# Second attention taken by pairs of heads, its output chunks moved behind all query, key and value chunks

## The reference, cut to what matters

```
def _chunk_attention(h, w_in, rel_bias, w_out):
    q, k, v = jnp.split(h @ w_in, 3, axis=-1)          # 16 heads of 64
    ...
    for each chunk of 64 queries, over a band of its own and the 8 chunks before it:
        s = einsum(q, k) * 64 ** -0.5 + bias           # relative bias, then a mask
        p = softmax(s)
        o = einsum(p, v)
    return o @ w_out
```

## Time and profile before

| | |
|---|---|
| median of 3 runs | 2123.19 us (2122.43 to 2123.32) |
| the profiled execution's own time | 2123.3 us |
| its span, first to last instruction | 2121.5 us |
| PE busy | 2039.8 us, 96% of the span |
| DVE, ACT, POOL busy | 937.8, 769.7 and 935.2 us (44%, 36%, 44%) |
| mean granted clock of TensorE | 0.986 of full speed |

### The profile page before, as it was taken

One profiled execution on the slowest core, in us unless ns is written; L12 is line 12 of the kernel. 1 busy time (PEld: TensorE's weight loads), 2 busy tenths in 40 slices (PEclk: granted clock), 3 DMA queues, 4 the chain that ended last, 5 costly groups with the idle time before them and its releaser, 6 DMA issues.

```text
span 2121.5 us, 24830 instructions
## 1 busy us (share of the span) xinstructions
PE 2039.8 (96%) x9710; PEld 1702.8 (80%) x9710; DVE 937.8 (44%) x1413; ACT 769.7 (36%) x1108; POOL 935.2 (44%) x680
## 2 busy tenths in 40 slices
PE   6988989999997999999999999999999989999998
PEld 5767768888886788888887888888888878888886
DVE  5477372323236754545545131325445555132233
ACT  5256442232233442424244232223444444232232
POOL 4440345555454435353535454555332214455552
PEclk9999999999998999999999999999999999999999
DMA  5340137466322323131322333323223203332321
GB/s 156 97 129 6 60 65 122 102 107 112 99 81 79 100 80 99 61 99 59 99 63 96 100 99 99 99 85 112 84 77 96 79 21 99 99 99 91 94 92 59
DMA packets 170016, 188.58 MB, mean 89 GB/s; under 512 B 4168, under 2 KB 158544, under 8 KB 169808
## 3 DMA queue, kind: packets, MB, share of 16 engines
q1 hardware_dynamic: 167648, 182.07, 26.9%
q10 hardware_dynamic: 1904, 4.59, 4.3%
q0 software_dynamic: 384, 0.81, 0.2%
HBM read 180.77 MB, written 4.72 MB: 87 GB/s over the span
## 4 chain that ended last, share of the span: by engine, by line
PE 71%; issue 15%; POOL 9%; DVE 3%; ACT 2%; DMA 0%; SPq 0%; POOLq 0%; ACTq 0%; DVEq 0%
PE ps L557 23%; PE ps L559 22%; PE ps L558 22%; POOL w_lo L527 9%; PE ps L708 1%; PE ps L719 1%; DVE hn_lo L1491 0%; DMA o_buf<-in_x 0%; PE ps L592 0%; DVE scr L1466 0%; PE ps L966 0%; DVE x L1840 0%; DVE hn_lo L1845 0%; ACT w_hi L977 0%; DVE scr L1698 0%
## 5 line engine op out<-in xcount | busy, mean ns | idle before, releaser
L527 POOL TENSOR_TENSOR w_lo<-raw,w_hi 128x512 fp32r<-128x512 f32 x652 | 916.9, 1437 | 1142.0 <-ACT w_hi L977 1142.0
L557 PE MATMUL ps<-hn_hi,w_hi 128*128 128x512 f32 x1504 | 600.4, 399 | 25.6 <-DVE hn_lo L1491 10.5
L559 PE MATMUL ps<-hn_hi,w_lo 128*128 128x512 f32 x1504 | 589.3, 392 | 0.0
L977 ACT ACTIVATE w_hi<-raw 128x2048 fp32r<-128x2048 f32 x163 | 312.4, 1917 | 762.9 <-PE ps L559 755.6
L558 PE MATMUL ps<-hn_lo,w_hi 128*128 128x512 f32 x1504 | 589.0, 392 | 0.0
L557 PE MATMUL ps<-hid_hi,w_hi 128*128 128x512 f32 x920 | 362.1, 394 | 5.3 <-issue 1.5
L557 PEld LDWEIGHTS ps<-hn_hi,w_hi 128*128 128x128 f32 x1504 | 284.4, 189 | 100.0 <-issue 22.1
L559 PE MATMUL ps<-hid_hi,w_lo 128*128 128x512 f32 x920 | 359.1, 390 | 0.0
L558 PE MATMUL ps<-hid_lo,w_hi 128*128 128x512 f32 x920 | 359.0, 390 | 0.0
L558 PEld LDWEIGHTS ps<-hn_lo,w_hi 128*128 128x128 f32 x1504 | 284.7, 189 | 61.4 <-issue 3.8
L559 PEld LDWEIGHTS ps<-hn_hi,w_lo 128*128 128x128 f32 x1504 | 284.5, 189 | 60.1
(11 more groups left out here) (222 smaller groups left out, 1986.8 us busy)
## 6 DMA issues: line engine op xcount, KB each, us to landing
raw<-in_mlp_w SPq DMA_DIRECT2D x64, 1024.0 KB, 5.3
raw<-in_ret_w_in SPq DMA_DIRECT2D x24, 1024.0 KB, 5.2
raw<-in_att_w_in SPq DMA_DIRECT2D x12, 1024.0 KB, 5.3
raw<-in_w_gate SPq DMA_DIRECT2D x11, 1024.0 KB, 5.4
raw<-in_w_up SPq DMA_DIRECT2D x11, 1024.0 KB, 5.4
raw<-in_w_in SPq DMA_DIRECT2D x8, 1024.0 KB, 5.7
raw<-in_w_down SPq DMA_DIRECT2D x8, 1024.0 KB, 8.7
raw<-in_ret_w_out SPq DMA_DIRECT2D x8, 1024.0 KB, 5.1
```

What stands on the lines that cost most here:

```text
L527: ins = pool.tensor_tensor(w_lo[:, slot, at], raw[:, slot, at], w_hi[:, slot, at].bitcast(F32), ALU.subtract)
L557: pe.matmul(o, hi, rhs_hi, start=start, stop=False, skip_group_check=True)
L559: return pe.matmul(o, lo, rhs_hi, start=False, stop=stop, skip_group_check=True)
L977: act.activation(w_hi[:, c.slot, :], raw[:, c.slot, :], ACT.Copy).then_inc(s["w_hi_ready"], 1)
```

## The change

The output chunks move behind all others: q0 k0 v0 q1 k1 v1 q2 k2 v2 q3 k3 v3 o0 o1 o2 o3. The heads are worked in pairs, eight pairs. The 14 chunks from v0 on are cut into 56 quarters of twelve matmuls of 512 columns (24 of 256 in a value chunk); pair p has its six phases ahead of the quarters 3 + 6p to 8 + 6p:

| phase | PE, ahead of that quarter |
|---|---|
| 0 | scores of the tiles 3, 2, 0 of both heads |
| 1 | scores of tile 1 of both heads |
| 2 | nothing |
| 3 | transposes of the first head |
| 4 | values of the first head, transposes of the second |
| 5 | values of the second head |

The two heads of a pair stand on partitions 0 to 63 and 64 to 127, and their score matmuls take turns, each into a bank of its own. In the values a head's weights are now its high part in 64 columns and its low part in the other 64, so that two matmuls a tile are made where there were three; the two halves of the result have to be added, by an ACT copy to the other half's partitions (`pair_shift`) and a DVE addition (`pair_sum`). ACT and DVE have their steps, the splits of the chunks among them, in the order of the phases. The biases are loaded two heads at a time. The scaled queries and keys go to `rstd` and to the place of `ext`, so that `scr` is free for the scores of two heads; some outputs go to `probs_t` and `hn_hi`. The first attention is as it was.

```diff
-ATT_ORDER = [(kind, g) for kind, g in zip("qkvqkvqkvoqkvooo", (0, 0, 0, 1, 1, 1, 2, 2, 2, 0, 3, 3, 3, 1, 2, 3))]
+ATT_ORDER = [(kind, g) for kind, g in zip("qkvqkvqkvqkvoooo", (0, 0, 0, 1, 1, 1, 2, 2, 2, 3, 3, 3, 0, 1, 2, 3))]
+ATT_FIRST, ATT_EVERY = 3, 6
+        EARLY, LATE = (3, 2, 0), (1,)
# TensorE
+            def pair_scores(p, tiles):
+                a = PAIRS[p]
+                if tiles is EARLY and a.half == 0:
+                    pe.wait_ge(s["att_in_lo"], a.group * 4 + 4)
+                for t in tiles:
+                    if tiles is LATE:
+                        pe.wait_ge(s["two_mx"], 8 * p + 2)
+                    elif p and t == 3:
+                        pe.wait_ge(s["two_lo"], 8 * p)
+                    elif p and t == 2:
+                        pe.wait_ge(s["two_o"], 2 * p)
+                    for n in range(3):
+                        for b in range(2):
+                            q, k = a.qk(b)[n]
+                            ins = pe.matmul(a.score_ps(b, t), q[:, t * P:(t + 1) * P], k[:, 0:(t + 1) * P],
+                                            start=(n == 0), stop=(n == 2), skip_group_check=True)
...
+            def pair_values(p, b):
...
+                for n, (j, subtracted) in enumerate(V_ORDER[b]):
+                    pe.wait_ge(s["two_lo"], 8 * p + 4 * b + subtracted)
+                    o, v = a.out_ps(b)[:, j * P:], a.v_both(b, j)
+                    pe.matmul(o, v, a.pt(0, j), start=(n == 0), stop=False, skip_group_check=True)
+                    ins = pe.matmul(o, v, a.pt(1, j), start=False, stop=(n == 3), skip_group_check=True)
...
+            for quarter in range(ATT_QUARTERS):
+                p, phase = pair_at(quarter)
+                if 0 <= p < ATT_PAIRS:
+                    if phase == 0:
+                        pair_scores(p, EARLY)
+                    if phase == 1:
+                        pair_scores(p, LATE)
+                    if phase == 3:
+                        pair_transposes(p, 0)
+                    if phase == 4:
+                        pair_values(p, 0)
+                        pair_transposes(p, 1)
+                    if phase == 5:
+                        pair_values(p, 1)
+                att_quarter(2 + quarter // 4, quarter % 4)
# ScalarE
+                if phase == 0 and p and p != 6:
+                    pair_out_hi(p - 1)
+                if phase == 1:
+                    if even:
+                        group_ready(ATT.group(ATT.upto[j]))
+                        take(j)
+                    pair_exps(p, 0)
+                    pair_exps(p, 1)
+                if phase == 3:
+                    pair_prob_hi(p, 0)
+                    if p == 6:
+                        pair_out_hi(5)
+                    next_split(quarter - 2 if even else quarter)
+                if phase == 4:
+                    pair_prob_hi(p, 1)
+                    if not even:
+                        take(1 + (quarter - 1) // 4)
+                if phase == 5:
+                    pair_shift(p, 0)
+                    pair_shift(p, 1)
+                    if even:
+                        next_split(quarter)
+                        take(j)
# VectorE
+                if phase != 1 and phase != 4:
+                    add_quarter(quarter - 1)
+                if phase == 0:
+                    pair_masked(p, EARLY)
+                if phase == 1:
+                    pair_masked(p, LATE)
+                    pair_negated(p, 0)
+                    pair_negated(p, 1)
+                    if p and p != 6:
+                        pair_out_lo(p - 1)
+                    take(j)
+                    add_quarter(quarter - 1)
+                if phase == 2:
+                    pair_probabilities(p, 0)
+                if phase == 3:
+                    if not even:
+                        scale(j)
+                    pair_prob_lo(p, 0)
+                    if p == 6:
+                        pair_out_lo(5)
+                    pair_probabilities(p, 1)
+                if phase == 4:
+                    pair_prob_lo(p, 1)
+                    if not even:
+                        take(1 + (quarter - 1) // 4)
+                    add_quarter(quarter - 1)
+                if phase == 5:
+                    if even:
+                        scale(j)
+                    pair_sum(p, 0)
+                    pair_sum(p, 1)
```

More of the change, by code:

```diff
@@ L930, in _ @@
-            att_product(0, act_wait=normed(N_ATT))
+                    if n == 0:
+                        pe.wait_ge(s["two_olo"], 2 * four + 2)
+                    g = ATT.group(ATT.upto[j] + n)
+                    hi, lo = (ap[:, c.slot, :].rearrange("p (k c) -> p k c", k=2) for ap in (w_hi, w_lo))
+                    group_empty(g)
+                    for k, a in enumerate(PAIRS[2 * four:2 * four + 2]):
+                        for m in range(2):
+                            at = slice((2 * n + m) * P, (2 * n + m) * P + P)
+                            ins = three(ps[:, g.bank(m), :], hi[:, k, at], lo[:, k, at], a.out(0), a.out(1),
+                                        k == 0, k == 1)
@@ L931, in _ @@
+                    ins.then_inc(s["group_done"], 1)
+                else:
+                    product(c, g, KD, 256, 0, hn_hi, hn_lo, None, range(2 * n, 2 * n + 2), n == 0, n == 3)
+            chunk_ready(ATT.chunk(0))
+            product(ATT.chunk(0), ATT.group(0), KD, 256, 0, hn_hi, hn_lo, normed(N_ATT))
             stat_columns(N_ATT)
             stat(N_ATT)
[L933 to L960, removed]
+            chunk_ready(ATT.chunk(1))
@@ new lines, in _ @@
+            product(ATT.chunk(1), ATT.group(1), KD, 256, 0, hn_hi, hn_lo)
+            for quarter in range(ATT_QUARTERS):
[13 more added lines that the diff above has]
+                att_quarter(2 + quarter // 4, quarter % 4)
@@ L1436, in _, with pair_exps @@
             take(1)
[L1437 to L1446, removed]
+            def pair_exps(p, b):
+                a = PAIRS[p]
+                act.wait_ge(s["two_nmx"], 2 * p + b + 1)
+                for t in range(4):
+                    col = slice(4 * b + t, 4 * b + t + 1)
+                    act.activation(a.score_sb(b, t), a.score_sb(b, t), ACT.Exp, bias=nmx[:, col],
+                                   accum_out=sm[:, col]).then_inc(s["two_exp"], 1)
@@ new lines, in pair_out_hi, with next_split @@
+            def pair_out_hi(p):
+                if p == 5:
+                    act.wait_ge(s["group_done"], ATT.group(ATT.upto[ATT_ORDER.index(("v", 3))]).done)
+                act.wait_ge(s["two_o"], 2 * p + 2)
+                act.activation(PAIRS[p].out(0), o_sum, ACT.Copy).then_inc(s["two_ohi"], 1)
+            def next_split(quarter):
+                j = 1 + quarter // 4
+                group_ready(ATT.group(ATT.upto[j + 1] - 1))
+                split(ATT.chunk(j + 2) if j < 14 else MLP_B.chunk(0))
@@ new lines, in _ @@
+            for quarter in range(ATT_FIRST, ATT_FIRST + ATT_EVERY * ATT_PAIRS):
+                p, phase = pair_at(quarter)
+                j = 1 + quarter // 4
+                even = p % 2 == 0
+                if phase == 0 and p and p != 6:
[21 more added lines that the diff above has]
+                        take(j)
@@ L2064, in _ @@
+            pair_out_lo(ATT_PAIRS - 1)
+            for quarter in range(ATT_FIRST + ATT_EVERY * ATT_PAIRS - 1, ATT_QUARTERS - 4):
+                add_quarter(quarter)
             for n in range(4):
```

317 lines of the change are left out of this document (206 added, 111 removed).

## The result

| | before | after |
|---|---|---|
| median | 2122.81 us (4 runs, 2122.12 to 2123.32) | 2085.81 us (4 runs, 2083.77 to 2088.40) |
| ratio after to before | | 0.9827, 95% interval 0.981 to 0.9844 |
| span of the profiled execution | 2121.5 us | 2083.8 us |
| k0 to the second MLP | 265.8 us, clock 0.98 | 227.7 us, clock 1.00 |

The kernel is 37.0 us faster by the medians and 37.7 by the spans. The attention is 38.1 us shorter; the rest of the span is 0.4 longer.

The account below looks back on a forecast made before the run. The prediction took PE, busy 96% of the span, as the bound. Its terms -13.7 - 10.2 - 9.2 + 1 + 3 = -29.1 us took 2123.3 to a forecast of 2094 us, range 2084 to 2107.

Parts of the forecast that it names:

- tail: Attention's last part, from 1695.43 on: waits and half clock of four heads with little beside them would go, -13.7 us.
- values: Value matmuls on PE: two for three in each key tile, 0.64 us a head over sixteen heads, -10.2 us.
- scores: Score matmuls of a pair's two heads, taking turns between row halves: partly side by side, -9.2 us.
- case B: Scores: matmuls side by side, weight loads one after another, 3.1 us a pair, saving 9.2 us; chance 0.38.
- insertions: Attention work enters the products 40 times instead of 32, each about 0.1 us late: +1 us.
- new waits: PE waiting in the pairs' new order: 0.3 us a pair plus one delay of 0.8, +3 us.
- Case A: Scores: both heads fully side by side, 2.3 us a pair, saving 15.4 us, time 2088; chance 0.24.
- C: Scores: nothing side by side, 4.2 us a pair, saving nothing, time 2103.4; chance 0.20.
- Rival 3: Attention: the softmax chain becomes the bound, waits of 18.4 us in place of 3, time 2109.6; chance 0.12.
- Rival 4: Scores: changing halves drains PE, 0.19 us for each of 192 matmuls, 36.5 us, time 2139.9; chance 0.04.
- The signs: Attention stretch 230 to 243 us, clock 1.00, no PE wait above 1 us, eight value matmuls a head in about 1.35.

Follow-up runs that it names:

- e3: The changed kernel with the last head's values after quarter 51 instead of before quarter 50, so nothing stands between them and output chunk o3; 2092.14 us.
- e2: The changed kernel with a third matmul for each key tile in the values, the low part once more; 2093.84 us.
- e1: The changed kernel with all of the first head's score matmuls in a section before all of the second's, without turns; 2097.91 us.
- e6: The changed kernel with the second head's scores reading the first head's 64 partitions, turns and banks kept; 2100.51 us.
- e4: The changed kernel with the transposes of a pair's first head one quarter earlier, in phase 2; 2129.39 us, ratio 1.0048 to the kernel before the change.
- e1b: The changed kernel with score matmuls tile by tile, three of the first head and then three of the second; 2084.82 us.
- e5: The changed kernel with, in pair 6, the low part of pair 5's output made after the second head's probabilities instead of before; 2083.87 us.
- e8: The changed kernel with POOL making only the first of the four parts of every low weight chunk; 2068.79 us.

## Why the prediction was right, step by step

| term | predicted | measured |
|---|---|---|
| tail | -13.7 | -13.7, by the idle time and clock that are gone |
| values | -10.2 | 16 x (1.27 - 1.99) = -11.5 |
| scores | -9.2 (case B) | 16 x 2.12 to 8 x 2.27: -15.8 |
| insertions | +1 | +1.9, by the starts of the products |
| new waits | +3 | +1.0 |
| sum | -29.1 | -38.1; the attention -38.1, the span -37.7 |

- **Tail.** Right: the attention's clock is 1.00 in both parts, and e3 shows what a chain without cover costs.
- **Values.** Right. The spacing gave 0.64 a head (e2: the same). The other 0.08 is the change to the 64-row form, which used to follow each head's values and now follows a product: e2's three matmuls a tile take 1.90 us without it, where they took 1.99.
- **Scores.** That the halves run side by side was right, and the size was off: the step that failed is "Two loads make 0.22 a step", with its 3.1 us a pair. Two loads and two matmuls of 128 columns fit in 0.11 us, and a pair takes 2.27. The spacing of matmuls on one half bounds that half alone. Case A, the first rival, is what happened: 2.27 us a pair against its 2.3, and with it the forecast would have been 2088. The prediction gave A 0.24 and B 0.38. Also, its "8 x 1.1 = 9.2" does not come out as printed: 8 x 1.1 is 8.8, and from 4.24 - 3.07 it is 9.4, which moves the forecast by under 0.5 us. The Trainium skill (TensorE: Matmul & The Clock Gate, Part 3: Packing small matmuls) says that matmuls on different row groups run at the same time and that their weight loads overlap; the x2 rows of the changed kernel agree, loads included. In the same section the Trainium skill says that matmuls start and end strictly in program order; the row at 1536.91 of e1 does not agree, and the measurement decides.
- **Insertions.** Too small by 0.9: after a score section the twelve matmuls take 2.94 us and after values or transposes 2.85, where twelve alone take 12 x 0.227 = 2.72. Of the 1.9 us 0.8 lie in the value chunks, which the prediction did not look at.
- **New waits.** The slack ahead of the first head's transposes was put at 0.7 us and at nothing in case A. Case A happened, and the probabilities still end 0.7 to 0.8 us ahead in six pairs (0.06 in two): the softmax chain starts at the end of the late scores, so it comes earlier together with PE, and faster scores take nothing from the slack. The one delay beside the output chunks was put at 0.8 us and is 0.86 to 1.0, but not by the additions that the prediction named: a low part of an output stands ahead of the multiplications there, and the last of them is held up by POOL. That the sizes agree is luck.
- **Rivals.** C is out by e6. Rival 3 did not happen, but its price was too low: e4, one quarter away from the change, is slower than the kernel before it. The prediction priced a lost slack at 18.4 us; e4 shows 46.5, since a shifted order also meets POOL. Rival 4, a drain at each change of halves, is out: 24 changes a pair cost nothing in sight. The 0.31 us between heads 12 and 13 fit the wait for DVE, as the weight load of that matmul shows:
```profile
1700.65 0.18 PEld L708 LDWEIGHTS ps<-hid_hi 64*128 64x128 f32 x1 [0.24 <-DVE small L1698]
```
- **The signs.** Of what would show it right, the clock, the largest wait (0.86 us) and the eight value matmuls (1.27 us a head) came as said. The stretch from k0 to the MLP did not: 227.7 us, below the 230 to 243. The time was inside its range because the range had been drawn to hold case A; the forecast itself was 8 us off, most of it in the scores.

## What to carry to other kernels

Matmuls with a contraction of 64 ran two at a time here when they stood on different halves and came within about three of one another (each half wrote to a bank of its own; one bank for both was not tried); bound what such a pair can do by the pace of one half, not of the whole engine. Give the last dependent chain work of its own length to hide behind: an uncovered one here cost 4.2 us of waiting and 1.7 of clock. Before an order written by hand is shifted, see in the timeline what each VectorE instruction will lie beside, not only how much time it has, and which of the two starts first.

## What the runs showed of the hardware

- **The two halves are fed ahead of program order.** The second half's first matmul started with three earlier ones of the first half still to come (e1); three and three ran as three (e1b: 18 matmuls in 1.71 us).
- **VectorE's multiplication by a column, from SBUF to SBUF, and POOL's subtraction hold each other up, and the one that starts second takes longer.** Behind POOL, four multiplications take 4.49 us in place of 1.27 (e4), and one that starts 0.01 us too late takes 1.54 in place of 0.48 (the changed kernel, pair 6). Ahead of POOL they keep their time, and POOL's instruction takes 1.53 to 1.63 in place of 1.27. A few ns are not told apart by these records: in e5 the slow one of pair 3 starts within 0.01 us of POOL. VectorE's subtraction with an operand in PSUM is not held up: in the changed kernel 8 of the 16 of 512 columns lie wholly beside POOL and take 0.69 us, as the other 8 do. The means of both in e4:
```profile
L2245 DVE TENSOR_SCALAR scr<-scr,small 128x512 f32<-128x512 f32 x16 | 11.7, 731 | 0.0
L2252 DVE TENSOR_TENSOR probs_t<-ps,probs_t 128x512 fp32r<-128x512 f32 x16 | 11.0, 688 | 6.9 <-ACT probs_t L1567 6.9
```
The first row's mean was 482 ns before the change. The Trainium skill (GPSIMD Engine Reference, 1. Specifications) names VectorE instructions in a two-port mode and those with two SBUF inputs as the ones that contend with GpSimd. For the second kind the rows of line 2143 agree (1614 ns, and 688 with a quarter of POOL's work in e8); no row tells the mode of an instruction, so whether the multiplication is of the first kind is not shown.
